# Two-layer attention trunk: score blocks in ascending order, layer two's probabilities laid by key block

## What is computed

```python
for layer in range(2):
    u = rmsnorm(h, norm_g[layer])
    h = h + (dsa_mixer(u, ...) if layer == 0 else dilated_mixer(u, ...))
return rmsnorm(h, final_g)
# both mixers, for each of 16 heads of width 128:
#   s = q @ k.T * 128 ** -0.5, masked;  p = softmax(s);  o = p @ v
#   y = (o * silu(z)) @ w_out
# dsa_mixer: one k and one v for all heads, each query keeps its 128 best keys
# dilated_mixer: k and v of each head, three dilated windows, mixed by their softmax weights
```

## Time and profile before

| | us |
|---|---|
| runs of the kernel, median of 3 | 945.88 (944.14 to 946.63) |
| the profiled execution, its own time | 945.93 |
| its span, first to last instruction | 944.1 |
| PE busy, share of the span | 925.9, 98% |
| DVE busy | 606.9, 64% |
| POOL busy | 564.0, 60% |
| ACT busy | 423.7, 45% |
| granted TensorE clock, mean | 0.996 |

### The profile page before, as it was taken

The page is one execution under the profiler, slowest core; times in us unless marked ns, Lnnn a source line. Parts: engine busy times, 40 slices in busy tenths (PEclk is TensorE's granted clock), DMA queues, the critical chain, the costliest instruction groups (busy, mean ns, idle before and its releaser), DMA issues.

```text
span 944.1 us, 13320 instructions
## 1 busy us (share of the span) xinstructions
PE 925.9 (98%) x4931; PEld 805.4 (85%) x4931; DVE 606.9 (64%) x1245; ACT 423.7 (45%) x772; POOL 564.0 (60%) x395
## 2 busy tenths in 40 slices
PE   6999999999999999999999999999999999999996
PEld 6798888888888888888898898989898988988886
DVE  4899798666656641146776666667768666665226
ACT  6664522455445543253443535452533434454323
POOL 2775544555555544456666677666766667774535
PEclk9999999999999999999999999999999999999998
DMA  8521323111211123221222222222222222132312
GB/s 306 154 92 68 112 90 107 50 45 45 68 45 45 49 86 112 90 89 67 68 90 90 90 76 76 72 90 88 70 69 88 91 90 90 53 104 88 113 44 90
DMA packets 25136, 81.48 MB, mean 86 GB/s; under 512 B 2928, under 2 KB 5232, under 8 KB 25072
## 3 DMA queue, kind: packets, MB, share of 16 engines
q1 hardware_dynamic: 23920, 79.57, 25.3%
q10 hardware_dynamic: 1152, 1.06, 0.3%
HBM read 78.52 MB, written 2.10 MB: 85 GB/s over the span
## 4 chain that ended last, share of the span: by engine, by line
PE 94%; DVE 3%; issue 1%; POOL 1%; DMA 0%; ACT 0%; POOLq 0%; ACTq 0%; DVEq 0%
PE ps L329 17%; PE ps L331 17%; PE ps L330 17%; PE ps L464 6%; PE ps L466 6%; PE ps L465 6%; PE ps L364 3%; PE ps L363 3%; PE ps L362 3%; PE ps L410 2%; PE ps L411 2%; PE ps L409 2%; PE ps L424 2%; PE ps L445 1%; PE ps L446 1%; PE ps L456 1%
## 5 line engine op out<-in xcount | busy, mean ns | idle before, releaser
L1299 POOL TENSOR_TENSOR w_lo<-w_raw,w_hi 128x1024 fp32r<-128x1024 f32 x137 | 338.1, 2473 | 180.1 <-ACT w_hi L648 178.6
L329 PE MATMUL ps<-u_hi,w_hi 128*128 128x512 f32 (+1 forms) x728 | 285.4, 392 | 9.7 <-DVE u_lo L950 7.3
L331 PE MATMUL ps<-u_hi,w_lo 128*128 128x512 f32 (+1 forms) x728 | 281.5, 387 | 0.0
L330 PE MATMUL ps<-u_lo,w_hi 128*128 128x512 f32 (+1 forms) x728 | 281.2, 386 | 0.0
L329 PEld LDWEIGHTS ps<-u_hi,w_hi 128*128 128x128 f32 x728 | 137.7, 189 | 35.5 <-issue 7.5
L331 PEld LDWEIGHTS ps<-u_hi,w_lo 128*128 128x128 f32 x728 | 137.3, 189 | 26.6
L330 PEld LDWEIGHTS ps<-u_lo,w_hi 128*128 128x128 f32 x728 | 137.8, 189 | 24.7 <-issue 0.2
L648 ACT ACTIVATE w_hi<-w_raw 128x1024 fp32r<-128x1024 f32 x138 | 143.5, 1052 | 27.1 <-DMA w_raw<-weights 18.0
L1087 DVE STREAM_TRANSPOSE bias_a<-probs 32x320 f32<-32x320 f32 x240 | 120.7, 503 | 18.4 <-POOL probs L1340 15.3
L1340 POOL TENSOR_SCALAR probs<-probs,inv_den 128x512 f32<-128x512 f32 (+3 forms) x128 | 66.2, 536 | 86.9 <-DVE inv_den L1076 86.8
L739 ACT ACTIVATE probs<-neg_s,neg_max 128x512 f32<-128x512 f32 (+3 forms) x128 | 70.4, 551 | 55.7 <-DVE neg_max L1069 55.0
(11 more groups left out here) (170 smaller groups left out, 1716.2 us busy)
## 6 DMA issues: line engine op xcount, KB each, us to landing
w_raw<-weights SPq DMA_DIRECT2D x138, 512.0 KB, 3.3
gated<-x_rows SPq DMA_DIRECT2D x4, 512.0 KB, 7.5
h<-x_turned SPq DMA_DIRECT2D x7, 256.0 KB, 5.9
outT<-h SPq DMA_DIRECT2D x10, 128.0 KB, 1.9
outT<-h ACTq DMA_DIRECT2D x6, 128.0 KB, 2.2
w_raw<-weights SPq DMA_DIRECT2D x2, 256.0 KB, 4.7
table<-rope_tables SPq DMA_DIRECT2D x2, 256.0 KB, 7.1
table<-rope_tables SPq DMA_DIRECT2D x1, 512.0 KB, 8.6
```

The lines of the kernel that those rows point to most:

```text
L329: pe.matmul(out, w_hi[:, g % SLOTS, blk], u_hi[:, k, tokens], start=(at == 0), stop=False)
L330: pe.matmul(out, w_hi[:, g % SLOTS, blk], u_lo[:, k, tokens], start=False, stop=False)
L331: last = pe.matmul(out, w_lo[:, g % SLOTS, blk], u_hi[:, k, tokens], start=False, stop=(at == KT - 1))
L1299: pool.tensor_tensor(w_lo[:, g % SLOTS, :], w_raw[:, g % 2, :], w_hi[:, g % SLOTS, :].bitcast(F32), ALU.subtract).then_inc(w_lo_ready, 1)
```

## The change

1. `scores`, `mask_scores` and `exps` go through the query blocks in the order 0, 1, 2, 3 instead of 3, 2, 1, 0, in both layers. Blocks 0 and 1 share a PSUM bank, and the mask of block 0 now waits until block 1's scores are there too.
2. For n = 16 to 30 POOL's `normalise` is replaced by `order`: it multiplies as before, but writes into `ordered`, which is the memory of `neg_s`, with the blocks in the order of `T_OFF`. It needs six instructions for it, table `GROUPS`, of which three write two blocks with a step between them.
3. `turn_blocks` reads `ordered`. `mask_scores`, which writes `neg_s`, waits for the transposes; `exps`, which writes `probs`, waits for POOL instead of for the transposes.
4. `output_by_parts` becomes `output_of_pair`: four products, 12 matmuls, over whole ranges of `pT_hi` and `pT_lo`. `CUT` is `T_OFF[2]` = 896, so the pieces of `turned_hi` and `turned_lo` have 896 and 384 columns.

```diff
@@ -89,8 +89,8 @@
 
 
 VECTOR_HEADS = range(HEADS, 2 * HEADS - 1)
-CUT = OFF[3]
-PARTS = (((0, 2, 0, 1), (2, 2, 3, 3)), ((1, 2, 2, 2), (3, 1, 7, 1)), ((2, 2, 5, 3),), ((3, 1, 9, 1),))
+CUT = T_OFF[2]
+GROUPS = (((0, 1, 0, 1),), ((0, 2, 1, 3),), ((0, 2, 2, 3), (2, 1, 7, 1)), ((0, 2, 3, 3), (2, 2, 8, 1)))
 
 
 def turned_before(n):
@@ -168,6 +168,8 @@
         left = neg_s[:, 0:COLS - P]
 
         turned = bias_a
+
+        ordered = neg_s
 
 
         gain = sb("gain", [P, 3 * KT])
@@ -400,16 +402,17 @@
 
             def scores(n, hi, lo, r):
                 pe.wait_ge(rope_lo_ready, r + 1)
-                for kk, i in enumerate((3, 2, 1, 0)):
+
+                for i in range(QB):
                     if n:
-                        pe.wait_ge(scores_read, n * QB - QB + (1, 2, 4, 4)[kk])
+                        pe.wait_ge(scores_read, n * QB - QB + max(i, 1) + 1)
                     at = 2 * P if i == 0 else 0
                     out = ps[:, S_BANK + max(i, 1) - 1, at:at + (i + 1) * P]
                     qs, ks = slice(i * P, (i + 1) * P), slice(0, (i + 1) * P)
                     pe.matmul(out, hi[:, qs], k_hi[:, ks], start=True, stop=False)
                     pe.matmul(out, hi[:, qs], k_lo[:, ks], start=False, stop=False)
                     last = pe.matmul(out, lo[:, qs], k_hi[:, ks], start=False, stop=True)
-                    if i != 1:
+                    if i:
                         last.then_inc(scores_done, 1)
 
             def turn_probs(n):
@@ -424,7 +427,7 @@
                             last = pe.transpose(ps[:, T_BANK + b, at:at + P], probs[:, src:src + P], ident[:, :])
                     last.then_inc(probs_turned, 1)
 
-            def output_by_parts(n):
+            def output_of_pair(n):
 
                 pe.wait_ge(gated_ready, n)
                 pair, head = divmod(n - HEADS, 2)
@@ -432,18 +435,14 @@
                 for x in (n_of(G_B + 8 * pair + 2), n_of(G_B + 8 * pair + 3)):
                     pe.wait_ge(bank_read[BANK[x]], TURN[x] + 1)
                 number = turned_before(n)[1]
-                for j, parts in enumerate(PARTS):
-                    vs = slice(j * P, (j + 1) * P)
+                for j in range(QB):
+                    pe.wait_ge(turned_lo_ready, 2 * number + (1 if T_OFF[j] < CUT else 2))
+                    out = ps[:, T_BANK, j * P:SEQ]
+                    vs, cols = slice(j * P, (j + 1) * P), slice(T_OFF[j], T_OFF[j] + SEQ - j * P)
                     high, low = pair_hi[:, head, vs], pair_lo[:, head, vs]
-                    for i, count, block, step in parts:
-
-                        pe.wait_ge(turned_lo_ready, 2 * number + (1 if block + (count - 1) * step < 6 else 2))
-                        out = ps[:, T_BANK, i * P:(i + count) * P]
-                        hi, lo = (t[:, :].rearrange("p (b c) -> p b c", c=P)[:, block:block + (count - 1) * step + 1:step, :]
-                                  for t in (pT_hi, pT_lo))
-                        pe.matmul(out, high, hi, start=(j == 0 and i == 0), stop=False)
-                        pe.matmul(out, high, lo, start=False, stop=False)
-                        last = pe.matmul(out, low, hi, start=False, stop=(i + count == QB and j == QB - 1))
+                    pe.matmul(out, high, pT_hi[:, cols], start=(j == 0), stop=False)
+                    pe.matmul(out, high, pT_lo[:, cols], start=False, stop=False)
+                    last = pe.matmul(out, low, pT_hi[:, cols], start=False, stop=(j == QB - 1))
                 last.then_inc(o_done, 1)
 
             def output(n, high, low):
@@ -543,7 +542,7 @@
                     project(tile + 3)
                 else:
                     values(tile + 2)
-                output_by_parts(n)
+                output_of_pair(n)
 
             def begin_blocks(t, blocks):
                 wait_for_head(1, t)
@@ -730,11 +729,12 @@
             def exps(n):
                 by_tensor, by_vector = turned_before(n)
                 if by_vector:
-                    act.wait_ge(blocks_turned, by_vector)
+
+                    act.wait_ge(probs_ready, n * QB)
                 elif by_tensor:
                     act.wait_ge(probs_turned, by_tensor * 3)
-                for kk, i in enumerate((3, 2, 1, 0)):
-                    act.wait_ge(scores_read, n * QB + kk + 1)
+                for i in range(QB):
+                    act.wait_ge(scores_read, n * QB + i + 1)
                     cols = slice(OFF[i], OFF[i] + (i + 1) * P)
                     act.activation(probs[:, cols], neg_s[:, cols], ACT.Exp, bias=neg_max[:, i:i + 1], scale=-1.0,
                                    accum_out=den[:, i:i + 1]).then_inc(exp_done, 1)
@@ -1057,13 +1057,13 @@
                     dve.match_replace(part, top8[:, i - 1, :], part, CHOSEN).then_inc(top8_taken, 1)
 
             def mask_scores(n, bias, offset):
-                for kk, i in enumerate((3, 2, 1, 0)):
-                    if i:
-                        if n:
-                            dve.wait_ge(exp_done, n * QB + kk + 1 - QB)
-                        dve.wait_ge(scores_done, n * 3 + kk + 1)
-                    elif n:
-                        dve.wait_ge(exp_done, n * QB)
+                if turned_before(n)[1]:
+
+                    dve.wait_ge(blocks_turned, turned_before(n)[1])
+                for i in range(QB):
+                    if n:
+                        dve.wait_ge(exp_done, n * QB + i + 1 - QB)
+                    dve.wait_ge(scores_done, n * 3 + max(i, 1))
                     at = 2 * P if i == 0 else 0
                     width = (i + 1) * P
                     dve.tensor_tensor_reduce(neg_s[:, OFF[i]:OFF[i] + width],
@@ -1081,7 +1081,7 @@
                 if number:
                     dve.wait_ge(turned_hi_ready, 2 * number)
                     dve.wait_ge(turned_lo_ready, 2 * number)
-                source, target = (t[:, :].rearrange("p (b c) -> p b c", c=P) for t in (probs, turned))
+                source, target = (t[:, :].rearrange("p (b c) -> p b c", c=P) for t in (ordered, turned))
                 for rows_at in range(0, P, 32):
                     for cols_at in range(0, P, 32):
                         last = dve.transpose(target[cols_at:cols_at + 32, :, rows_at:rows_at + 32],
@@ -1340,6 +1340,18 @@
                     pool.tensor_scalar(probs[:, cols], probs[:, cols], inv_den[:, i:i + 1], 1.0, ALU.mult,
                                        ALU.mult).then_inc(probs_ready, 1)
 
+            def order(n):
+
+                pool.wait_ge(inv_ready, n + 1)
+                blocks = ordered[:, :].rearrange("p (b c) -> p b c", c=P)
+                for i in (3, 2, 1, 0):
+                    for first, count, place, step in GROUPS[i]:
+                        cols = slice(OFF[i] + first * P, OFF[i] + (first + count) * P)
+                        last = pool.tensor_scalar(blocks[:, place:place + (count - 1) * step + 1:step, :],
+                                                  probs[:, cols].rearrange("p (b c) -> p b c", c=P),
+                                                  inv_den[:, i:i + 1], 1.0, ALU.mult, ALU.mult)
+                    last.then_inc(probs_ready, 1)
+
             def turned_lo(n):
                 number = turned_before(n)[1]
                 pool.wait_ge(o_done, n)
@@ -1361,7 +1373,7 @@
             def head_b(hd):
                 n, tile, r = HEADS + hd - 1, G_B + 4 * hd, R_B + 2 * hd
                 if hd:
-                    normalise(n)
+                    order(n)
                     split_w(tile + 2)
                     split_w(tile + 3)
                     turned_lo(n)
```

## The result

The changed kernel takes 963.85 us (962.21 to 965.14), the kernel before 945.94 in the same runs: a ratio of 1.0188, 95% interval 1.0177 to 1.0199. The forecast was 942.5, and the range ended at 945.6.

A forecast was written before the change was run, and what follows sets the result against it. The prediction took PE, busy 98% of the span, to bound the kernel. Outputs -3.0 and order of scores -0.4, all else hidden, gave -3.4 on 945.93: 942.5 us, own range 941.4 to 944.6, 8-in-10 range 941.2 to 945.6.

The forecast's parts named there:

- Outputs, -3.0 us: PE's output matmuls, n = 16 to 30: four products take 1.86 us instead of six pieces' 2.06, saving 0.20 a head.
- n = 30: Exceptional head: its scores already wait for `k_lo`; POOL's extra 0.53 is covered, the wait may grow by 0.0 to 0.3.
- Order of scores, -0.4 us: PE's score matmuls, ascending: zero in layer two, -0.04 us a head in layer one from joints; -1.3 to +0.8 possible.
- POOL's multiplication, +0.53: POOL's six instructions instead of four: two more starts cost +0.53 us, writes into distant blocks nothing extra; hidden from PE.
- My two rivals about `order`: POOL's `order` paying blocks like instructions, +1.6, 947.4 us, chance 0.10; or slow as two-input work, +2.55, 961, chance 0.05.
- The second of them: POOL becomes the bound: `order` takes 4.6 us, +2.55, PE waits before the next scores; 961 us, chance 0.05.
- Exponentials, 0.2 us earlier: ACT's exponentials, layer two: ascending, the last block and its sum end at 687.32, so the inverse comes 0.2 us earlier.
- the time that `k_lo` has to spare: POOL's lead in handing over the next key's low part before PE's next scores: 0.46 us n even, 1.1 n odd.
- the cut at 896 ... `turned_lo` starts that much later: ACT's first piece is 128 columns longer, delaying `turned_lo` by 0.11 us; its two pieces keep 1280 columns and 3.55 us.

The follow-up runs named there:

- 958.5: The kernel before with CUT at 896 and nothing else (the PE wait moved to match): 958.49 us, ratio 1.0135.

## Why the prediction was wrong

**Outputs, -3.0 us: right but for one head.** In the changed kernel the last twelve matmuls before the scores of n = 26 take 1.86 us from 720.07, with 0.11 for the last, and the four products have the pitches of layer one.

```profile
720.07 0.40 PE L443 MATMUL ps<-pT_hi,q_hi 128*128 128x512 f32 x1
...
721.82 0.27 PE L445 MATMUL ps<-pT_hi,q_lo 128*128 128x128 f32 x1
```

With CUT 768 the stretch from the first scores of n = 16 to those of n = 31 takes 388.7 us instead of 391.4. That is 2.7 and not 3.0, mainly because n = 30 gains nothing, 25.87 us against 25.86: its next scores wait for `k_lo`, as the prediction saw, but the sum counted the head all the same. The six kernels without the key's stall or an added wait have medians of 943.3 to 944.0, 0.2% to 0.3% below the one before and within the forecast's own range.

**Order of scores, -0.4 us: size off, the term is about zero.** Layer one gained nothing, 10.39 us a head in both orders. In layer two the scores up to the projection's second matmul take 2.20 us descending. Ascending they take 2.24 in the changed kernel, the figure that the expectations above use, but there they stand right behind a wait; with CUT 768 they take 2.18 to 2.21, and two heads in a row 51.85 us against 51.83 descending. Without this term the sum would have been 942.9, and without n = 30 943.1.

**POOL's multiplication, +0.53: right.** Its six instructions take 2.54 us instead of 2.06. In the changed kernel's groups two blocks of 128 columns take 479 ns in `order` (three of the four with the blocks written apart) and 480 in layer one's `normalise`, so writes into distant blocks cost nothing extra. My two rivals about `order` did not happen. The second of them named 961 us and waits at the right place, `k_lo`; but `order` is far from the 3.8 us that it needed, so its nearness to the result is chance.

```profile
701.11 2.54 POOL L1350 TENSOR_SCALAR neg_s<-probs,inv_den 128x256 f32<-128x256 f32 x6 [4.55 <-DVE inv_den L1076]
```

**Exponentials, 0.2 us earlier: right for n even, wrong for n odd.** Counted from the head's first score, they end at 4.15 us before. With CUT 768 they end at 3.84 for n even and at 4.38 for n odd. For n odd they begin at 2.09 instead of 1.86, since the table load behind the gates is no longer done in time; n = 25 with CUT 768:

```profile
682.38 1.28 ACT L800 ACT_TABLE_LOAD   x1
683.68 0.40 ACT L739 ACTIVATE probs<-neg_s,neg_max 128x128 f32<-128x128 f32 x1
```

It is hidden as said, but the time that `k_lo` has to spare is 0.73 us for n even and 0.80 for n odd, where 0.46 and 1.1 were forecast.

**The step that failed is "the cut at 896 ... `turned_lo` starts that much later".** I priced the cut by its owner alone, 0.11 us of ACT's time, and took POOL's and DVE's instructions to last as long as in the rows before. By that reckoning the spare time was enough, 0.46 us and 1.1. In truth the cut set when DVE's next addition could get through, and through that who was first 3.5 us later. The rows that showed it were at hand: line 1012 took 1.26 and 0.73 us for the same shape in one head, and line 1299 2.85 and 2.4. I asked of neither why. Against the kernel with CUT 768 the loss adds up. With the split ahead of the key's addition, `k_lo` ends 10.87 us behind the transposes instead of 9.91, 1.0 later. Less the 0.73 to spare, this costs heads of n even 0.3 us (25.62 to 25.93). For n odd the transposes themselves end 2.1 us later behind the head's first score (17.67 instead of 15.53), together 3.1, less 0.80: 2.4 with roundings (26.23 to 28.60). Seven heads of each and 1.0 for n = 30 are the 20 us.

**What stays open.** That the two inputs in SBUF are what makes the two engines exclude each other was seen by contrast (lines 1007 and 1008 run undisturbed beside POOL) and agrees with what the Trainium skill says; no run moved an input of the addition to PSUM. The recorded spans of POOL are rough, so the leads of 0.07 and 0.06 us are no exact threshold; what carries the step is that the order of the two changes with the 20 us. How the difference between 958.5 and 963.9 divides between `order` and the rest was not tried.

## What to carry to other kernels

When the same instruction in the same shape has two durations in a trace, find out who holds it up before moving anything near it: a lead of 0.15 us over the other engine was worth 20 us here, and a changed split point, or 0.27 us of harmless work, turned it around. A spare time holds only as long as nobody's durations change; ask of each moved instruction who will arrive at a shared port in front of whom. If an order between two engines matters, write it down as a wait (945.1 us with the bad cut) or leave a wide lead (0.43 us with CUT 640) instead of trusting a race, and size pieces so that a waiting instruction gets its turn at their boundary.

## What was unexpected of the hardware

- The loss is a step: 943.4 us with the addition 0.07 us ahead of the split, 963.0 with it 0.06 behind, in all 15 heads of either trace. The eight runs of the one kernel lie within 2.9 us and the two of the other within 1.2, so the race falls the same way from run to run.
- DVE standing at POOL shows as a longer duration, not as idle time: busy DVE grew by 36 us, and neither engine's list of waits names the other for it.
- A 128-column matmul costs 0.11 us wherever it stands. Alternated with large ones it takes 0.06 itself, and the 384 columns behind it 0.23 instead of 0.17.
